# Encoder layer on one core: another order of products, taps and sums at the entry of the up projection, and of values and weighing in the attention

## What is computed

```python
h = _rmsnorm(x, norm1) @ w_in
c_q, c_kv, k_rope, u = h[..., :o1], h[..., o1:o2], h[..., o2:o3], h[..., o3:]
q = jnp.einsum('bsr,rhd->bshd', _rmsnorm(c_q, q_a_norm), w_q_b)
kv = jnp.einsum('bsr,rhd->bshd', _rmsnorm(c_kv, kv_a_norm), w_kv_b)
attn = _attend(q_nope, q_rope, k_nope, k_rope, v)        # 8 heads, softmax over 512 keys
pool = _multiscale_pool(u, pool_w, pool_scale)
x = x + jnp.concatenate([attn, pool], axis=-1) @ w_out
up = _dwconv3(_rmsnorm(x, norm2) @ w_up, conv_w, conv_b)
gate, val = up[..., :D_FF], up[..., D_FF:]               # D_FF = 2816
x = x + (jax.nn.silu(gate) * val) @ w_down
g = jax.nn.sigmoid(_rmsnorm(x, norm3) @ w_ple_gate + b_ple_gate)
x = x + (p @ w_ple_proj) * g                             # and a last rmsnorm
```

## Time and profile before

| | |
|---|---|
| median of 3 runs | 1203.74 us (1200.92 to 1464.96) |
| the profiled execution | 1203.63 us, its span 1201.6 us |
| TensorE busy (PE) | 1155.6 us, 96% of the span, 5252 matmuls |
| VectorE busy | 787.7 us, 66% |
| ScalarE busy | 530.8 us, 44% |
| GpSimd busy | 303.6 us, 25% |
| TensorE's granted clock, mean | 0.982 of full speed |
| the chain that ended last | PE 86%, DVE 8%, ACT 2%, issue 2%, POOL 1% |

### The profile page before, as it was taken

How to read it: one execution, slowest core, us unless ns; L and a number is a source line. 1 busy time by engine, 2 the same in 40 slices (tenths; PEclk the granted TensorE clock), 3 DMA queues, 4 the chain that set the end, 5 groups by cost and what they waited for, 6 DMA issues and landing times.

```text
span 1201.6 us, 16001 instructions
## 1 busy us (share of the span) xinstructions
PE 1155.6 (96%) x5252; PEld 926.9 (77%) x5252; DVE 787.7 (66%) x1104; ACT 530.8 (44%) x910; POOL 303.6 (25%) x299
## 2 busy tenths in 40 slices
PE   6999889999999979999999999999999999999996
PEld 4887666665788757888888888888888888888885
DVE  5649777655359698777777777877333564348665
ACT  5411577766223354545444454544323343325342
POOL 0138523232457123322333223320000020002100
PEclk7999899999999999999999999999999999999999
DMA  6520000003652216231313223133544444433341
GB/s 198 196 55 17 11 12 12 23 14 118 222 203 94 74 34 225 82 105 52 105 57 100 90 67 105 52 105 117 180 133 155 134 155 135 153 114 105 100 144 72
DMA packets 121332, 123.98 MB, mean 103 GB/s; under 512 B 7155, under 2 KB 103754, under 8 KB 119498
## 3 DMA queue, kind: packets, MB, share of 16 engines
q1 hardware_dynamic: 120992, 123.33, 31.3%
q10 hardware_dynamic: 298, 0.11, 0.0%
HBM read 98.25 MB, written 25.17 MB: 103 GB/s over the span
## 4 chain that ended last, share of the span: by engine, by line
PE 86%; DVE 8%; ACT 2%; issue 2%; POOL 1%; DMA 0%; DVEq 0%; SPq 0%; POOLq 0%; ACTq 0%
PE ps L260 26%; PE ps L262 26%; PE ps L261 26%; PE ps L697 2%; PE ps L678 2%; DVE WDHL L1617 1%; PE ps L572 1%; PE ps L689 1%; ACT SF L1092 1%; DVE col L1628 1%; DVE CHL L1743 1%; DVE SF L1860 0%; PE ps L550 0%; DVE SF L1852 0%; DVE XL L1478 0%
## 5 line engine op out<-in xcount | busy, mean ns | idle before, releaser
L260 PE MATMUL ps<-XH,WH 128*128 128x512 f32 x728 | 291.5, 400 | 12.5 <-DVE WL L1748 5.2
L262 PE MATMUL ps<-XH,WL 128*128 128x512 f32 x728 | 285.4, 392 | 0.0
L261 PE MATMUL ps<-XL,WH 128*128 128x512 f32 x728 | 285.3, 392 | 0.0
L290 ACT ACTIVATE WH<-WR 128x1024 fp32r<-128x1024 f32 (+1 forms) x89 | 92.2, 1035 | 304.0 <-PE ps L262 295.6
L295 DVE TENSOR_TENSOR WL<-WR,WH 128x1024 fp32r<-128x1024 f32 (+1 forms) x89 | 115.6, 1299 | 147.1 <-ACT WH L290 146.7
L260 PEld LDWEIGHTS ps<-XH,WH 128*128 128x128 f32 x728 | 137.9, 189 | 44.2 <-issue 13.3
L260 PE MATMUL ps<-GHL,WH 128*128 128x512 f32 x436 | 169.8, 389 | 0.3 <-DVE SF L1860 0.3
L261 PE MATMUL ps<-GHL,WH 128*128 128x512 f32 x436 | 169.6, 389 | 0.0
L262 PE MATMUL ps<-GHL,WL 128*128 128x512 f32 x436 | 169.6, 389 | 0.0
L261 PEld LDWEIGHTS ps<-XL,WH 128*128 128x128 f32 x728 | 138.0, 190 | 29.8 <-issue 2.2
L262 PEld LDWEIGHTS ps<-XH,WL 128*128 128x128 f32 x728 | 137.8, 189 | 29.1
(11 more groups left out here) (214 smaller groups left out, 1975.0 us busy)
## 6 DMA issues: line engine op xcount, KB each, us to landing
WR<-in_w_down SPq DMA_DIRECT2D x44, 512.0 KB, 3.5
TL<-in_w_up SPq DMA_DIRECT2D x48, 256.0 KB, 3.8
g_scratch<-SF SPq DMA_DIRECT2D x22, 512.0 KB, 4.5
SF<-g_scratch SPq DMA_DIRECT2D x44, 256.0 KB, 3.6
WR<-in_w_up SPq DMA_DIRECT2D x40, 256.0 KB, 3.1
WR<-in_w_out SPq DMA_DIRECT2D x16, 512.0 KB, 3.9
XT<-xt_scratch SPq DMA_DIRECT2D x8, 1024.0 KB, 6.8
WR<-in_w_ple_gate SPq DMA_DIRECT2D x16, 512.0 KB, 3.6
```

The costliest lines, as they stand in the source:

```text
L260: pe.matmul(out, wh, xh, start=first, stop=False, skip_group_check=skip)
L261: pe.matmul(out, wh, xl, start=False, stop=False, skip_group_check=skip)
L262: return pe.matmul(out, wl, xh, start=False, stop=last, skip_group_check=skip)
L290: act.activation(WH[:, slot(n), base:cols, :], WR[:, slot(n), base:cols, :], ACT.Copy).then_inc(w_hi, 1)
```

## The change

Attention: `values(i, 1)` of pairs 1 to 3 moves from round 0 of its pair to round 14 of the pair before, with one more wait (rr_copied, ScalarE's copy of the row scales out of bank 7), and its copy on ScalarE from round 1 to round 15 of the pair before, ahead of `q_split`. The second half of `weigh(i, 0)` moves from round 14 to round 12 in all pairs. Entry of the up projection: the `spread` comes ahead of `whole(1)` instead of after its first three tiles; ScalarE's `up_hi(S2)` comes ahead of the first silu; VectorE's low halves of quarters 1 and 0 come ahead of all eight taps of the first block and S2's right behind them, and the taps are no longer interleaved with other work; GpSimd's `up_sums(1, 0)` waits in addition for b_lo 32, the last entry tile.

```diff
--- before.py
+++ after.py
@@ -642,6 +642,7 @@
                 bank = 7 if i else 4 + s
                 if i and s:
                     pe.wait_ge(v_copied, i * 2 + 1)
+                    pe.wait_ge(rr_copied, i * 2 - 1)
                 elif i >= 2:
                     pe.wait_ge(rr_copied, i * 2 - 2)
                 for t in range(TT):
@@ -717,8 +718,6 @@
                     elif not last:
                         scores(i + 1, u + 3 - 4 * TT)
 
-                    if u == 0 and i:
-                        values(i, 1)
                     if u == 1 and i:
                         project_q(i, 3, k_lo, i * 4 + 4)
                     elif u == 1:
@@ -729,7 +728,7 @@
                         weigh(i - 1, 1, (2, 3))
                     if u == 10:
                         weigh(i, 0, (0, 1))
-                    if u == 14:
+                    if u == 12:
                         weigh(i, 0, (2, 3))
                     if not last:
                         if u == 5:
@@ -742,6 +741,8 @@
                             project_q(i + 1, 1, k_lo, i * 4 + 6)
                         if u == 13:
                             project_q(i + 1, 2, qf_ready, i * 4 + 6)
+                        if u == 14:
+                            values(i + 1, 1)
                         if u == 15:
                             project_k(i + 1, 1, qf_ready, i * 4 + 7)
 
@@ -896,9 +897,8 @@
                 ins = pe.matmul(ps[6][:, TT + t:TT + t + 1], SQT[:, t * P:(t + 1) * P], ones[:, 0:1], start=False, stop=True)
             ins.then_inc(ss_ready, 1)
             whole(0, range(2, KT))
-            whole(1, range(0, 3))
             spread(B_X2 + 1, 5)
-            whole(1, range(3, KT))
+            whole(1)
             entry("1")
             whole(2)
             whole(3)
@@ -1313,8 +1313,8 @@
             up_hi(quarter(0, 0), raw_in[0][0], 64, m_done, entry_at("7"), 0)
             for c in range(1, 4):
                 whole_centre(c)
+            up_hi(S2, ws_ready, 10, m_done, entry_at("3"), 1)
             silu(0, 0, 0)
-            up_hi(S2, ws_ready, 10, m_done, entry_at("3"), 1)
             silu(0, 0, 1)
             gate0(0, 1, False)
             up_hi(s1_buf(0), ws_ready, 9, m_done, entry_at("4"), 2)
@@ -1888,20 +1888,15 @@
             up_lo(quarter(1, 3), 2, 14)
             for k in range(2, 4):
                 piece_lo("4", k, xt[:, 0, 4 + k, :])
-            tap_left(0, 0, 0)
-            tap_right(0, 0, 0)
-            tap_left(0, 0, 1)
-            tap_right(0, 0, 1)
-            tap_left(0, 0, 2)
             up_lo(quarter(0, 1), 3, 15)
-            tap_right(0, 0, 2)
-            tap_left(0, 0, 3)
             up_lo(quarter(0, 0), 0, 16)
-            tap_right(0, 0, 3)
+            for c in range(4):
+                tap_left(0, 0, c)
+                tap_right(0, 0, c)
+            up_lo(S2, 1, 17)
             product(0, 0, 1)
             product(0, 0, 0)
             tap_left(0, 1, 0)
-            up_lo(S2, 1, 17)
             tap_right(0, 1, 0)
             up_lo(s1_buf(0), 2, 18)
             for c in range(1, 4):
@@ -2214,6 +2209,7 @@
                 squares(1, m, x2_ready, m + (KT + 1), m + (KT + 1))
             root(B_X2 + 1, 4, 5)
             pool.wait_ge(uw_lo, 13)
+            pool.wait_ge(b_lo, 32)
 
             def up_sums(i, f):
```

## The result

The changed kernel takes 1206.11 us (median of 20 runs, 1204.35 to 1207.23), the kernel before 1201.51 (median of 20, 1199.9 to 1204.18 but for one of 1464.96 that the comparison leaves out). The ratio is 1.0034, 95% interval 1.0026 to 1.0041: slower by some 4 us, far inside 2%. Both kernels' times lie in two groups: before 1199.9 to 1202.0 and 1203.5 to 1204.2, changed 1204.4 to 1204.7 and 1206.0 to 1207.2. This matters here since the profiled execution of before (1203.63) is of its upper group, that of the changed kernel (1204.41, span 1202.4) of its lower one; how far the clock explains the groups is taken up at the end.

A forecast was written before the change was run, and what follows sets the result against it. TensorE bounds from the up loop's third product on, VectorE in the 56.3 us before. 1203.63 + 4.8 − 0.6 − 3.2 + 0.9 = 1205.5 us, range 1200.5 to 1209.5.

The forecast's parts named there:

- The values, +4.8: Round 1, pairs 1 to 3: project_q 1.6 us later at each of three boundaries, +4.8 us (3.8 to 5.1).
- Rival B: Attention: values covered nothing, project_q's chain shortens with TensorE; 1199.8 us, 1198.1 if the low stretch goes; chance 0.14.
- The weighing, −0.6: Earlier second half: 0 in pairs 0 to 2; last pair's diagonals start 0.6 earlier, −0.6 us (0 to −0.9).
- The entry, −3.2: Entry to up projection: earlier spread −0.8, GpSimd's wait −2.7, grouped taps +0.3, together −3.2 us.
- GpSimd's wait: Up projection entry: GpSimd starts after VectorE's low half and two tiles, which it had held up; −2.7 us.
- the spread: Up projection entry: spread ahead of whole(1), TensorE's nine steps take 2.05 us instead of 2.86; −0.8 us.
- The grouped taps, +0.3: VectorE, b_lo 32 to the loop: grouped taps lose overlap, some 0.1 us each for three, +0.3 us.
- the 5.2 us: TensorE's longest wait, for VectorE's low half (L1748), would become four of 2.1, 0.5, 1.2 and 2.7 us.
- The two rules that spoke against it: Entry: VectorE's low halves contend with GpSimd; silu's table load, about 2.66 us with drain, would delay VectorE's product 0.8.
- The clock, +0.9: Three new waits in the attention bring half of one more half-clock stretch: +0.9 us (−1.7 to +5).
- rival A: Entry's gain lost to GpSimd's port lock, table-load drain or half-clock stretch behind "7": 1207 to 1208.7 us; chance 0.2.
- The base: Whole kernel: the sum starts from the profiled execution, 1203.63 us, said to be 0.1 below the median.

The follow-up runs named there:

- values alone: Kernel before with only the second sequence's values moved to round 14 (copy in round 15), weighing left in round 14: 1207.05 us, ratio 1.0039.
- both attention edits: Kernel before with the moved values and the earlier weighing, nothing changed at the up projection's entry: 1206.14 us, ratio 1.0040.
- the run with all waits filled: Changed kernel with two useless matmuls in the wait at product 7 and in each of three project_q waits of round 1: 1202.80 us, ratio 1.0011.

## Why the prediction was right, step by step

It named 1205.5 us and 1200.5 to 1209.5; measured 1206.11, no change beyond 2% as forecast. The mechanisms and most sizes of the work held. That the number came within 0.6 us is luck: the clock's term was too small and the base too high, and the two nearly cancelled.

- **The values, +4.8.** Three waits of 1.76 us where 0.13 had been, 1.6 each: measured +1.63 a boundary (1.76 less 0.13). The split into 1.28 of TensorE's order and 0.3 to 0.4 of ScalarE's copy shows in the two turned copies, counted with the 0.18 by which the attention started earlier: that of round 15 comes 1.30 later (185.11 against 183.99), that of round 0 1.64 (187.27 against 185.81). The chain was the one named. Rival B (the values covered nothing) is out. The prediction says that its range takes in the upper half of B; it doesn't, as B's times, 1199.8 and 1198.1, both lie below 1200.5.
- **The weighing, −0.6.** In the last pair 0.8 clean by values alone against both attention edits, and the wait for the diagonals 0.2. "0 in pairs 0 to 2" was right for this change, for a reason that the prediction didn't have (the longer wait covers it), and wrong by itself: 0.35 each without that wait.
- **The entry, −3.2.** Measured −3.1 clean. GpSimd's wait 2.6 (I had 2.7), the spread 0.86 (0.8). The grouped taps, +0.3 in my sum, are +0.35 on VectorE's path from the last tile to the loop (441.19 to 457.13 before, 440.08 to 456.37 now), but the same order spared a low half the hold-up by GpSimd, so beside GpSimd's wait it won 0.3. The waits that the 5.2 us would turn into were put at 2.1, 0.5, 1.2 and 2.7; they are 2.0, 0.2, 1.0 and 2.4. The two rules that spoke against it did not cost it anything. VectorE's low halves were issued first (440.00) and GpSimd's combination (440.22) took 2.23 us. The Trainium skill (SBUF — State Buffer, Who interferes with whom) says that issue order decides which of the two blocks, and the trace agrees with its 2.23 us. The table load took 1.28 us (444.50), the silu began as it ended (445.79), and VectorE's product came at 447.58 without a wait, so no drain beyond the load was on the path.
- **The clock, +0.9.** The mis-sized term. The profiled execution has a half-clock stretch behind the wait at product 7, which I had only as one case of rival A, and one in the attention, as have all four profiled kernels with these waits. The two are 3.4 us, not 0.9. So "from the 7 product on all as before" failed: 741.9 us to the end instead of 740.3.
- **The base.** I summed against the profiled execution of 1203.63 us and said that it stood at the median. It stood at the median of three runs; the median of twenty is 1201.51. It held two such stretches (250.5 and 397.3) itself, and twelve of the twenty runs, at 1199.9 to 1202.0, are faster by 1.6 to 3.7 us, where two stretches cost 3.4. Between the two profiled executions the clock's term is about 0, as each has two stretches: 1203.63 + 1.1 − 0.2 for the earlier start of the attention is 1204.5, and 1204.41 was measured. Counted from a run of before without a stretch (some 1200.2) the sum is 1200.2 + 1.1 + 3.4 = 1204.7, the lower group of the changed kernel. So the change costs the median run 4 to 4.6 us where my steps said 1.9: 1.1 of it is work moved, 1.6 the stretch behind product 7, and the rest, by the profiles and the run with all waits filled, most likely the clock as well, in the attention or at the place around 397.

That the lower group of before is made of runs without such stretches, or with one, is read from the times and the profiled executions, since only these have a trace; it wasn't shown run by run. The mean granted clock, which is on record for single runs, fits it for before: 0.982 to 0.984 in the runs above 1203.4, 0.986 to 0.992 in the others. Two stretches make only 0.003 of that; the rest is about what a long one at 11.5 to 25.2 us makes, which the profiled execution has too, and it left no mark on the start of the attention (151.63, against 151.36 to 152.36 in profiles without it).

What the upper group of the changed kernel (1206.0 to 1207.2, eleven of twenty runs) has more than the profiled one stays open. One further stretch would fit most of it, and the place at 394.9 to 401.4, where half of the profiles have one, is a candidate, but no profile of this group was taken, and its mean clocks (0.984 to 0.991, the lower group 0.990 to 0.991) don't tell.

## What to carry to other kernels

An operation that costs nothing where it stands may be the cover of a chain that leaves TensorE and comes back: before moving it, follow what TensorE issued ahead of it to the wait behind it, and count what the move puts into the other engines' part of that chain. Removing a long wait of TensorE ahead of the point that another engine sets only moves the idle time towards that point. Idle time just ahead of the stage where TensorE is the bound was the dear one here, as the clock's loss is paid there; two matmuls of no use in it gave that loss back. Read how many half-clock stretches the profiled execution holds before summing against its time.

## What the runs showed of the hardware

The granted clock fell to the 1.2 GHz level behind waits of TensorE of only 1.76 us (four of four kernels, behind one of three such waits each), 2.4 to 2.5 us (six of seven) and 1.60 us (two of the eight kernels without a wait of 1.3 us or more in round 1), in one profiled execution of each kernel and in kernels whose TensorE is busy some 96% of the span. Behind these waits the fall lasted 3.4 us each time, and at product 7 filling the wait with matmuls kept the clock at 1.00 in three of three profiles. I had counted half of one such fall for three waits together. It also fell, in seven of fourteen profiles, 1.8 to 2.9 us after the start of a group of one-column matmuls that had waited only 0.18 us.

VectorE and GpSimd, each with both inputs in SBUF, held each other up in both directions: VectorE's two tiles took 3.48 us instead of 1.28 with GpSimd's combinations ahead, GpSimd's combination 2.23 instead of 1.29 with VectorE's two low halves ahead. In these traces the one issued later paid.
